# A hybrid decoder step: two thirds of w_ada loaded and used between the w_in blocks, and the middle of the kernel in another order

## The reference, cut to what matters

```python
mod = silu(c) @ w_ada + b_ada                  # w_ada is 1024 x 6144, 25 MB
sh1, sc1, gt1, sh2, sc2, gt2 = split(mod, 6)
h = rmsnorm(x, g_mix) * (1 + sc1) + sh1
z = h @ w_in                                   # 1024 x 2816, 11.5 MB
q_a, k_a, v_a, q_h, f_h, i_h, g_h = split(z)
o_a = rmsnorm(sink_attention(rotary(q_a), rotary(k_a), v_a), g_attn_out)
f = lb + (1 - lb) * sigmoid(f_h)
o_h, S_new = hgrn(q_h, 1 - f, i_h, log(f))     # gated linear recurrence
o_h = rmsnorm(o_h, g_hg_out) * silu(g_h)
x = x + gt1 * (concat(o_a, o_h) @ w_out)
h = rmsnorm(x, g_ffn) * (1 + sc2) + sh2
x = x + gt2 * moe(h)                           # top 4 of 32 experts, 12.6 MB each
y = rmsnorm(x, g_final)
```

## Time and profile before

| | |
|---|---|
| median of 3 runs | 1176.32 us (1175.99 to 1177.31) |
| the profiled execution | 1177.35 us, of which the span of the core is 1175.6 us |
| TensorE busy | 1099.1 us (93%) |
| moved by DMA | 461.65 MB, 393 GB/s on average |
| mean granted TensorE clock | 0.997 of full speed |
| first expert matmul | at 241.48 us |

### The profile page before, as it was taken

How to read it: one execution, slowest core, us unless ns; L and a number is a source line. 1 busy time by engine, 2 the same in 40 slices (tenths; PEclk the granted TensorE clock), 3 DMA queues, 4 the chain that set the end, 5 groups by cost and what they waited for, 6 DMA issues and landing times.

```text
span 1175.6 us, 14105 instructions
## 1 busy us (share of the span) xinstructions
PE 1099.1 (93%) x5497; PEld 440.7 (37%) x5497; DVE 345.2 (29%) x761; ACT 162.9 (14%) x313; POOL 55.8 (5%) x86
## 2 busy tenths in 40 slices
PE   7999999999999999989898989898989898989896
PEld 3677756633333333233222323232323232322222
DVE  4154377431322213222222222222222212221214
ACT  3232171301010001000100010001000100000003
POOL 1140002010000000000000000000000000000000
PEclk9999999999999999999999999999999999999999
DMA  9881299999999999999999999999999999999994
GB/s 366 323 290 72 90 388 378 351 351 417 430 430 429 431 430 430 430 432 430 430 429 431 431 430 431 430 430 430 430 432 429 431 431 430 431 430 429 430 429 203
DMA packets 49128, 461.65 MB, mean 393 GB/s; under 512 B 6657, under 2 KB 7873, under 8 KB 22202
## 3 DMA queue, kind: packets, MB, share of 16 engines
q1 hardware_dynamic: 42512, 445.17, 90.7%
q0 software_dynamic: 5600, 13.13, 3.1%
q10 hardware_dynamic: 986, 2.95, 0.7%
HBM read 460.30 MB, written 5.78 MB: 396 GB/s over the span
## 4 chain that ended last, share of the span: by engine, by line
PE 57%; DMA 38%; DVE 3%; issue 1%; ACT 0%; SPq 0%; ACTq 0%; DVEq 0%
PE bank L1599 27%; DMA arena<-in_w_up 17%; DMA ring<-in_w_up 17%; PE bank L1479 6%; PE bank L1623 4%; DMA arena<-in_w_down 3%; PE bank L896 2%; PE bank L1392 2%; PE bank L1062 2%; PE bank L1592 2%; PE bank L1148 1%; PE bank L1011 1%; PE bank L1041 1%; PE bank L994 1%; PE bank L1132 1%; PE bank L1485 1%
## 5 line engine op out<-in xcount | busy, mean ns | idle before, releaser
L1599 PE MATMUL bank<-arena 128*64 128x512 f32 x1024 | 239.9, 600 | 12.1 <-DMA arena<-in_w_up 11.5
L1599 PE MATMUL bank<-ring,arena 128*64 128x512 f32 x1024 | 240.0, 601 | 9.7 <-DMA ring<-in_w_up 8.5
L1599 PEld LDWEIGHTS bank<-arena 128*64 128x64 f32 x1024 | 67.3, 136 | 165.1 <-issue 149.5
L1599 PEld LDWEIGHTS bank<-ring,arena 128*64 128x64 f32 x1024 | 66.0, 136 | 163.4 <-issue 137.6
L1623 PE MATMUL bank<-arena 128*64 128x512 f32 x512 | 114.6, 596 | 9.0 <-DMA arena<-in_w_down 9.0
L1623 PE MATMUL bank<-ring,arena 128*64 128x512 f32 x512 | 114.6, 596 | 8.9 <-DMA ring<-in_w_down 8.9
L2167 DVE TENSOR_SCALAR arena<-bank 128x256 f32<-128x256 f32 x64 | 24.1, 419 | 274.7 <-PE bank L1599 274.7
L1479 PE MATMUL bank<-arena,mods 128*128 128x512 f32 (+1 forms) x204 | 93.7, 630 | 0.9 <-DVE arena L2194 0.9
L850 ACT ACTIVATE arena<-arena 128x512 f32<-128x512 f32 x32 | 20.2, 630 | 493.0 <-DVE arena L2167 493.0
L2156 DVE TENSOR_TENSOR x<-x,bank 128x512 f32<-128x512 f32 x64 | 44.0, 687 | 144.5 <-PE bank L1479 144.5
L896 PE MATMUL bank<-const,arena 128*128 128x128 f32 (+3 forms) x348 | 51.1, 286 | 21.3 <-DMA ring<-in_w_down 7.6
(11 more groups left out here) (336 smaller groups left out, 802.0 us busy)
## 6 DMA issues: line engine op xcount, KB each, us to landing
ring<-in_w_up SPq DMA_DIRECT2D x64, 2048.0 KB, 34.1
arena<-in_w_up SPq DMA_DIRECT2D x64, 2048.0 KB, 34.3
ring<-in_w_down SPq DMA_DIRECT2D x32, 2048.0 KB, 33.7
arena<-in_w_down SPq DMA_DIRECT2D x31, 2048.0 KB, 33.4
ring<-in_w_ada SPq DMA_DIRECT2D x16, 1024.0 KB, 12.5
ring<-in_w_ada SPq DMA_DIRECT2D x16, 512.0 KB, 10.8
ring<-in_w_in SPq DMA_DIRECT2D x3, 2048.0 KB, 15.0
ring<-in_w_in SPq DMA_DIRECT2D x5, 1024.0 KB, 12.8
```

Of the source, the lines that this page charges most:

```text
L1599: mm = pe.matmul(B[2 * e + c % 2][64 * a:64 * a + 64, :], lhsT=xTe[:, k, 64 * e:64 * e + 64], rhs=big(PER * s + n)[:, r, 512 * c:512 * (c ...
```

## The change

It moves work, and computes the same. By engine:

- **SP.** Three chunks of w_ada stand directly behind the twelve chunks of f and q_h, then `Z4` and the attention's block, three more of w_ada, the i block, ten of w_ada, the g block. The place of each chunk comes from the table `PLACES`. The waits are new: the i block waits for `chunks_used` at 12, which the first matmul of `by_column("k")` gives, and w_ada's seventh chunk is listed behind it. Each of chunks 3 to 5 waits until a chunk three before it is used. The w_out chunks and the first expert chunk wait less.
- **TensorE.** `ada_chunk` 0 to 7 stand between the second half of the q_h columns and `by_column("v")`, 8 to 15 between the attention queries. `inner` takes the place of `by_token`: 512 columns at once, in two halves of the contraction, with levels 5 to 7 and the scores between. The g columns now stand among `turn_probs` and `values`. `modT2` and `modT3` stand together ahead of `head_squares(0)`; from there to `project(0)` there is no `ada_chunk`. `prow` and the first chunks of w_ada stand between the transposes of x, and `lbb` behind `turn_modulation(0)`.
- **VectorE and ScalarE** follow that order: masks and maxima of the scores between the levels, probabilities earlier; `norm_heads(1)` and `km` later than before.
- **GpSimd.** The eight loads of b_ada's rows come ahead of the states instead of behind the sinks.
- Some scratch places in the arena are others (`pbd`, `ps`, `pvr`; `squares_h` for `squares_a`).

The core of the diff:

```diff
+PLACES = (2, 3, 4, 5, 6, 7, 0, 1, 2, 3, 4, 5) + (1,) + (2, 3) + (4, 5) + (2, 3) + (
+    6, 7, 0, 6, 7, 0, 6, 7, 0, 1, 6, 7, 0, 1, 6, 7) + (6, 7, 4, 5)
...
-            return (n + 1) % RING
+            return PLACES[n]
...
-            for n in ZFIRST:
-                c, wide_ = ZORDER[n], z_wide(Z0 + n)
-                room(Z0 + n + wide_ - 1)
-                sp.dma_start(z_chunk(Z0 + n), w_in[:, :, c * ZC:(c + wide_) * ZC]).then_inc(full[place(Z0 + n)], 16)
-            for k in range(N_ADA):
-                room(ADA1 + k)
-                sp.dma_start(chunk(ADA1 + k), w_ada[k, :, CH:2 * CH]).then_inc(full[place(ADA1 + k)], 16)
...
+            def w_ada_rows(i):
+
+                n = ADA1 + i
+                if i < 3:
+                    sp.wait_ge(chunks_used, 5 + i)
+                elif i == 9:
+                    sp.wait_ge(chunks_used, Z0 + 5)
+                else:
+                    sp.wait_ge(ada_used, i - 2 if i < 9 else i - 3)
...
+            for i in range(3):
+                w_ada_rows(i)
+            w_in_columns(Z4, 8)
+            w_in_columns(Z0 + 5, 10)
+            for i in range(3, 6):
+                w_ada_rows(i)
+            w_in_columns(Z0 + 7, 12)
+            for i in range(6, 2 * N_ADA):
+                w_ada_rows(i)
+            w_in_columns(Z0 + 9, 15)
...
+            pool.wait_ge(sem("f_ready"), 2)
+            for q in range(2):
+                for j in range(4):
+                    n0 = (q + 1) * CH + j * 512
+                    pool.dma_start(ba[32 * j:32 * j + 9, q, :],
+                                   wide(A["b_ada"][0:1, n0:n0 + 512], 0, 9)).then_inc(sem("ada_rows_full"), 16)
             pool.wait_ge(chunks_used, N_ADA + 3)
...
             turn_modulation(0)
+            pe.wait_ge(sem("diag_ready"), 2)
+            out = take("lbb")
...
             queries_half(0, 1)
             decode_forget_half(1)
+            ada = take("ada2")
+            ada_chunk(0, ada)
             queries_half(1, 1, after=1)
+            ada_chunk(1, ada)
...
+            ada_chunk(2, ada)
             queries_half(2, 1)
+            ada_chunk(3, ada)
...
+            ada_chunk(4, ada)
             queries_half(3, 1)
+            ada_chunk(5, ada)
...
             by_column("k", Z0 + 4, 0, after=1)
+            ada_chunk(6, ada)
...
             by_column("v", Z0 + 4, P)
+            give(ada_chunk(7, ada), "ada2")
...
+            turn_rows_of("modT2", 1)
+            turn_rows_of("modT3", 2)
+            head_squares(0)
             row_squares("as1", 1, P, P)
...
             give(mm, "oT")
-            ada_chunk(ADA2, 4, ada)
             wait_emptied(pe, "dpv")
             out = take("dT")
             give(turn(out[:, 0:64], pvr[0:64, :], 64), "dT")
-            ada_chunk(ADA2, 5, ada)
...
+            wait_emptied(dve, "krow")
+            dve.tensor_tensor(km, wide(krows.unsqueeze(1), 1, NB), wide(C("same").unsqueeze(2), 2, P), ALU.mult).then_inc(sem("km_ready"), 1)
+            norm_values("as0", 0, P)
+            norm_heads(1)
+            norm_values("asd", S, NB).then_inc(sem("att_ready"), 1)
```

More of the change, by code:

```diff
@@ L980, in _ @@
             turn_modulation(0)
+            pe.wait_ge(sem("diag_ready"), 2)
+            out = take("lbb")
+            give(pe.matmul(out[:, :], lhsT=ones, rhs=lb_diag.rearrange("p h c -> p (h c)"), start=True, stop=True), "lbb")
             def prompt_half(name, n, half):
@@ L1263, in turn_probs, with values @@
                 give(mm, f"pT{i}")
-            pe.wait_ge(sem("probs_scaled"), 1)
-            turn_probs(0, 1, 0, 0)
-            turn_probs(1, 1, 1, 0)
+            def values(name, parts, after=0):
+                out = take(name)
+                for n, units in enumerate(parts):
+                    for g in range(KV):
+                        wait_emptied(pe, f"pT{units[g]}")
+                        mm = pe.matmul(out[64 * g:64 * g + 64, :], lhsT=vrow[:, n, 64 * g:64 * g + 64], rhs=pT[:, units[g], :],
+                                       start=(n == 0), stop=(n == len(parts) - 1), skip_group_check=True)
+                        if n == 0 and g == 0:
+                            release(mm, after)
+                give(mm, name)
@@ new lines, in head_squares, with row_squares @@
+            def head_squares(t):
+                pe.wait_ge(sem("hg_squares"), t + 1)
+                out = take(f"hs{t}")
+                give(pe.matmul(out[:, :], lhsT=ones, rhs=squares_h[:, :, P * t:P * (t + 1)], start=True, stop=True), f"hs{t}")
+            def row_squares(name, made, lo, n):
+                pe.wait_ge(sem("att_squares"), made)
+                out = take(name)
+                for j in range(GRP):
+                    mm = pe.matmul(out[:, 0:n], lhsT=ones, rhs=squares_t[:, j, lo:lo + n], start=(j == 0), stop=(j == GRP - 1))
+                give(mm, name)
@@ L1268, in _ @@
+            out = take("kd")
+            give(turn(out[0:NB, 0:P], qk[:, 4, S:NTOK], P), "kd")
+            decode_rows("id", Z0 + 7)
+            state(0)
+            recurrence(0)
             pe.wait_ge(sem("qbd_ready"), 1)
@@ L1426, in _ @@
             project(0)
-            wait_emptied(pe, "ada3")
-            out = take("modT3")
-            for b in range(4):
-                mm = turn(out[:, P * b:P * (b + 1)], mods[:, 2, P * b:P * (b + 1)], P)
-                if b == 0:
-                    mm.then_inc(ada_used, 1)
-            give(mm, "modT3")
             project(1)
@@ L1683, in _ @@
             ins.then_inc(sem("diag_ready"), 1)
-            for k in range(4, 6):
+            for k in range(4, KT):
                 take_x(k)
```

518 lines of the change are left out of this document (258 added, 260 removed), and 24 rows, old and new, of the table bank_of.

## The result

The changed kernel takes **1209.83 us** (median of 4 runs, 1208.33 to 1212.45), the kernel before beside it 1176.82 (4 runs, 1175.99 to 1180.75): a ratio of 1.0279, 95% interval 1.0263 to 1.0295, that is 33 us more. The prediction said 1194 us, at most 1203: the sign was right, the size was not. The profiled execution of the changed kernel took 1208.33 us; its core's span is 1206.5 us, 30.9 more than before.

A forecast was written before the change was run, and what follows sets the result against it. It took the long stage to be bound by the stream of expert weights. Its terms, -1.6 - 3.5 + 14 + 5.5 + 0.5 + 3 = +17.9 us, gave 1194 us; the forecast spanned 1183 to 1203, the range going down to 1179.

The forecast's parts named there:

- The bound: Long stage from 235 us to the end: bound by the stream of expert weights, at 417 to 432 GB/s.
- the shift: How far the first expert matmul moves; claimed to reach the end one for one.
- the prize: TensorE's waits in the first 241 us that a new order can remove: 4.7 us in all.
- the vanished waits: TensorE's waits ahead of the cumulative sums, for w_ada and for VectorE later: 3.5 us off (bounds 2 and 3.5).
- the cover: w_ada chunks ahead of project(0) that had hidden VectorE's work there; the change takes them away.
- The wait at `project(0)`: TensorE waits there for VectorE's work at the end of the front: 5.5 us (bounds 3 and 7).
- The wait among the probabilities: VectorE copies state and decode scores before scaling the first probabilities, with only g0 to cover: 0.5 us (bounds 0 and 2).
- The place of the longest wait: At w_ada's chunk 6, behind k, listed after the 2 MB i block: 8 to 9 us.
- New waits for w_ada: TensorE waits for late loads before chunks 3, 4, 5 and 6: 14 us (bounds 6 and 20).
- the end of the front: From the heads' sum to project(0): VectorE ends after 18.3 us, TensorE has 12.5 left; 5.5 us added.
- The front: lbb moves into TensorE's 1.2 us wait for VectorE, at a faster pace: 1.6 us off (bounds 1.0 and 1.9).
- The clock: Lower granted clock behind the long waits at chunk 6 and project(0): 3 us (bounds 0 and 5).

The follow-up runs named there:

- e6_three: Changed kernel with w_ada chunks 3 to 8 listed by need, GpSimd's states and caches loaded later, and modT3's bank emptied behind modT2's: 1184.84 us, ratio 1.0055.
- e12_tail: e6_three with the first heads' squares sum, its root and norm, the modT2 and modT3 transposes and copies, and norm_values(as0) moved earlier: 1180.79 us, ratio 1.0028.
- e3_bank: Changed kernel with one edit: VectorE empties modT3's bank right behind modT2's, not behind two of the norms: 1204.25 us, ratio 1.0233.
- e8_front_only: Kernel before with only the change's first part: prow and first w_ada chunks among the columns of x, lbb behind modT1a: 1178.44 us, ratio 1.0001.
- e7_busy_exact: Changed kernel with unread matmuls added: 5 ahead of chunk 3, 13 of chunk 6, 6 of the second od, 4 of project(0): 1208.36 us, ratio 1.0259.
- e9_tail_busy: e6_three with 5 unread matmuls added ahead of project(0), where TensorE waits for VectorE: 1182.13 us, ratio 1.0045.

## Why the prediction was right and wrong

**Right.** The bound, and that the shift passes to the end one for one. That the prize was small (the vanished waits, 3.5 us, did vanish) and the cover mattered: with nearly all new waits for loads gone, the change is still not faster (e6_three, e12_tail). The wait at `project(0)` (3.9 us for 5.5). The wait among the probabilities (0.4 for 0.5). The place of the longest wait, behind k, and its mechanism, a 2 MB block listed ahead: 6.8 us without GpSimd's loads, 6 by my sum.

**Wrong, by my steps.**

*New waits for w_ada*, 14 us: 17.7 measured (18.5 the second time). The pieces were 5.0 at chunk 3 for 3 to 4, 0.2 and 0.3 at chunks 4 and 5 for 2 together, and 12.2 at chunk 6 for 8 to 9. It landed at 93.2 us, not at 87 to 88. I had spread the megabytes evenly over the time from 60 us on (and counted 14 us from 44 to 60, which are 16; that would have made it 86). But SP could issue chunk 6 only at 78.4, not at 69.2, because k's first matmul, which the i block waits for, came at 77.3 behind chunk 3's wait; and from 75 to 85 us GpSimd's queue took the larger part of what moved, 1.98 of 3.1 MB:

```profile
q0 software_dynamic: 647, 1.98, 66.0%
q1 hardware_dynamic: 524, 1.09, 31.0%
```

It stays inside the bounds of the term (6 to 20).

*A wait that isn't in the sum*, and the step that failed most. 5.4 us at `od1`, for bank 7: I had put it at nothing. I costed every step that was moved on VectorE and TensorE, and not the new table of banks, though the diff shows it: `modT3` and `od1` in one bank, with the copy behind two norms. e3_bank measures it at 5.6 us. This alone would have put the sum at 1199.6. (The term for the end of the front was near, 3.9 for 5.5, though by its own parts it is 18.3 less 12.5, that is 5.8.)

*The front*, -1.6 us: 0 on average, at most 1.4 (e8_front_only). The row of `lbb` was right, but most of its 1.62 us ran at the slow pace of the first matmuls, which ends at another time in each profile.

*The clock*, +3 us: I priced two waits at 1.7 us each, and there were four places, with work at half speed taking some 9 us of the timeline. Its cost at the end is at least 1.5 to 5 us by e7_busy_exact, whose added matmuls held up two of the four places by 3.1 us themselves. So as a part of this timeline the term was too small by 6 us; as a cost its size stays open. Its picture, a clock that falls in a wait, was right at chunk 6 and not ahead of `project(0)`, the two places that I had priced.

*The sum.* The 31.7 us of the profile are 25.6 of waits and 6.1 of work. The latter is some +9 of half-speed work at the four places, -3.2 ahead of the f columns, mostly a pace that fell well in this execution, -1.2 at the gather (6.10 us for 7.31), and 1.5 more, of which 0.9 is `outer` ahead of `project(0)`, at half speed too (2.09 us for 1.17). My range ended at 1203 because I took the bounds of the terms that I had, and had no room for a term that I had missed.

**Open.** When the pace of the first matmuls doubles, and why the clock falls ahead of `project(0)` and at the gather, was seen and not explained. How much of the half-speed work is a cost at the end isn't settled, nor whether the new middle costs a microsecond by itself.

## What to carry to other kernels

Where a change comes with a table of buffers or banks, go through it as through the code: for each name, who used the place last, and what stands ahead of the copy that frees it. Loads that move into an idle gap need two looks, at the bytes of all queues in that gap and at the issuing engine's list, since a load stands behind the waits of all that are listed ahead of it; mending one of them here gave 6 to 10 us, both and the bank together 25. Where matmuls are added to fill a wait, look up afterwards when the load or the other engine was done: the filling may itself have become the wait. Work taken out of a stretch that hid another engine's chain turns into a wait there, however well the loads go.

## What the runs showed of the chip that I had not expected

- The first matmuls run at half pace until 14 us in one execution and until 24 us in another of the same kernel, while the granted clock is given as 1.00 in both; the f columns begin 3.0 us apart in these two.
- The granted clock can fall with TensorE busy: 0.51 from 212 to 214 us in the changed kernel, 1.99 of 2.00 us busy, ahead of any long wait. Where chunks of w_ada stood among the same small matmuls (before, 182 to 188 us) it was 1.00.
- The length of the wait ahead doesn't say how much work behind it is slow. The first two columns of the projection took 10.2 us to the next line behind 2.3 us of wait (e12_tail), 9.25 behind 4.4 (e6_three), 8.70 and 10.35 behind 3.9 (the changed kernel, twice), and 7.21 with TensorE kept busy (e9_tail_busy).
- The gather's 48 records follow the clock, with no edit near them: 6.10 us in five profiles, where the granted clock is 1.00 throughout; 6.36 to 6.65 in five and 7.31 to 7.72 in four, where it falls to 0.50 ahead of the gather or in it. The wait ahead of the router's sums is 1.8 us in all fourteen.
